# Three-pass fp32 feed-forward stages: 18 of 22 gate/up units as 2x2 block products with seven products for eight

## The reference, cut to what matters

```python
D_MODEL, SEQ, FFN_HIDDEN = 1024, 512, 2816

def swiglu(h, w1, w3, w2):
    return (jax.nn.silu(h @ w1) * (h @ w3)) @ w2
...
        h = modulate(rms_norm(x), sh2, sc2)
        x = x + g2[:, None, :] * swiglu(h, ffn_w1[layer], ffn_w3[layer], ffn_w2[layer])
```

## Time and profile before

| | |
|---|---|
| runs, us | 2479.25, 2486.27, 2486.68 |
| profiled execution, span, us | 2481.9 |
| PE busy | 2416.7 us, 97% of the span, 12256 matmuls |
| DVE, ACT, POOL busy | 1238.3 us (50%), 902.1 us (36%), 70.3 us (3%) |
| mean granted TensorE clock | 0.986 of full speed |
| DMA | 267.34 MB, mean 108 GB/s |

### The profile page before, as it was taken

One profiled execution on the slowest core, in us unless ns is written; L12 is line 12 of the kernel. 1 busy time (PEld: TensorE's weight loads), 2 busy tenths in 40 slices (PEclk: granted clock), 3 DMA queues, 4 the chain that ended last, 5 costly groups with the idle time before them and its releaser, 6 DMA issues.

```text
span 2481.9 us, 30237 instructions
## 1 busy us (share of the span) xinstructions
PE 2416.7 (97%) x12256; PEld 2022.5 (81%) x12256; DVE 1238.3 (50%) x1449; ACT 902.1 (36%) x1215; POOL 70.3 (3%) x81
## 2 busy tenths in 40 slices
PE   7989999999999999999999999999999999999998
PEld 6658888888799778888878888879989877888886
DVE  6677543356746543332254442346678545444423
ACT  3353333313344333332143332244556544333311
POOL 0210000000003000000000000000000000000000
PEclk9999999999999999999999999999999999999999
DMA  8116522364233122222222222221212212222221
GB/s 341 73 63 243 186 102 101 139 239 164 87 123 91 68 84 86 101 101 100 87 85 101 98 88 102 102 98 69 85 52 79 75 68 85 85 101 101 88 100 67
DMA packets 40549, 267.34 MB, mean 108 GB/s; under 512 B 4394, under 2 KB 5674, under 8 KB 9490
## 3 DMA queue, kind: packets, MB, share of 16 engines
q1 hardware_dynamic: 31248, 219.87, 24.6%
q0 software_dynamic: 5840, 40.37, 4.2%
q10 hardware_dynamic: 3378, 5.91, 0.9%
HBM read 263.90 MB, written 2.24 MB: 107 GB/s over the span
## 4 chain that ended last, share of the span: by engine, by line
PE 89%; DVE 6%; ACT 3%; issue 1%; DMA 0%; DVEq 0%; SPq 0%; ACTq 0%
PE bank L231 26%; PE bank L233 26%; PE bank L232 26%; DVE w_lo L218 1%; PE bank L2160 1%; ACT w_hi L214 1%; PE bank L2256 1%; PE bank L334 1%; PE bank L2243 1%; PE bank L1868 1%; DVE work L461 1%; DVE work L445 1%; PE bank L2231 1%; PE bank L1864 1%; ACT work L438 1%
## 5 line engine op out<-in xcount | busy, mean ns | idle before, releaser
L231 PE MATMUL bank<-h_hi,w_hi 128*128 128x512 f32 x1800 | 711.1, 395 | 5.3 <-DVE w_lo L218 2.0
L233 PE MATMUL bank<-h_hi,w_lo 128*128 128x512 f32 x1800 | 703.3, 391 | 0.0
L232 PE MATMUL bank<-h_lo,w_hi 128*128 128x512 f32 x1800 | 703.3, 391 | 0.0
L218 DVE TENSOR_TENSOR w_lo<-raw,w_hi 128x2048 fp32r<-128x2048 f32 x192 | 439.9, 2291 | 477.6 <-ACT w_hi L214 477.6
L214 ACT ACTIVATE w_hi<-raw 128x2048 fp32r<-128x2048 f32 x192 | 366.3, 1908 | 413.1 <-PE bank L233 409.6
L231 PEld LDWEIGHTS bank<-h_hi,w_hi 128*128 128x128 f32 x1800 | 339.5, 189 | 82.0 <-issue 6.7
L233 PEld LDWEIGHTS bank<-h_hi,w_lo 128*128 128x128 f32 x1800 | 339.4, 189 | 71.8
L232 PEld LDWEIGHTS bank<-h_lo,w_hi 128*128 128x128 f32 x1800 | 339.7, 189 | 70.6 <-issue 1.4
L233 PE MATMUL bank<-g_hi,w_lo 128*128 (+1 forms) x704 | 273.9, 389 | 0.0
L231 PE MATMUL bank<-g_hi,w_hi 128*128 (+1 forms) x704 | 273.9, 389 | 0.0
L232 PE MATMUL bank<-g_lo,w_hi 128*128 (+1 forms) x704 | 273.9, 389 | 0.0
(11 more groups left out here) (331 smaller groups left out, 2816.9 us busy)
## 6 DMA issues: line engine op xcount, KB each, us to landing
raw<-stream SPq DMA_DIRECT2D x192, 1024.0 KB, 4.8
work<-stream POOLq DMA_DIRECT2D x19, 1024.0 KB, 6.5
h_plain<-stream POOLq DMA_DIRECT2D x16, 1024.0 KB, 5.4
work<-stream SPq DMA_DIRECT2D x13, 1024.0 KB, 12.3
work<-mlstm_rows ACTq DMA_DIRECT2D x8, 512.0 KB, 4.8
x<-xT SPq DMA_DIRECT2D x1, 2048.0 KB, 10.5
outT<-work SPq DMA_DIRECT2D x8, 256.0 KB, 2.3
work<-mlstm_rows ACTq DMA_DIRECT2D x8, 192.0 KB
```

Source lines behind the costliest of these rows:

```text
L218: nc.vector.tensor_tensor(w_lo[:, slot(m), :], raw[:, slot(m), :], w_hi[:, slot(m), :], ALU.subtract).then_inc(lo_split, 1)
L231: nc.tensor.matmul(out, stationary[0], moving[0], start=first, stop=False)
L232: nc.tensor.matmul(out, stationary[0], moving[1], start=False, stop=False)
L233: return nc.tensor.matmul(out, stationary[1], moving[0], start=False, stop=last)
```

## The change

The first four gate/up units (`FFN_WHOLE`) stay as they are. In the other 18 of each stage the 128 gate columns and the 128 up columns, the even and the odd chunks of the 1024 features, and the two halves of the tokens (256 and 256) make a 2x2 by 2x2 block product. It is computed by a scheme with seven products (Winograd's form) instead of eight. A product is 4 chunks x 3 passes = 12 matmuls of 256 columns.

- **Sums of h**, five per stage, each 128 x 4 x 256, plus in ffn2 and ffn3 eight multiplications of x by the gain: on POOL, in place in `t` (`FeedForward.gpsimd`). They start when h (or x) is complete. ACT and DVE split the result into `t_hi_tile` and `t_lo_tile` (`hidden_high`, `hidden_low`), behind unit 0's work in their queues.
- **Sums of weights**, four per unit: two by an accumulating DMA that POOL issues (`add_parts`, 512 KB added to 512 KB loaded in `mixes`), two by DVE (`make_further`). SP issues three DMAs per unit instead of one (512, 256 and 512 KB).
- **Splits**: three weight blocks from raw (`whole_high`, `whole_low`, 1536 columns), two from `mixes` and two from `further` (1024 columns each). `w_hi` and `w_lo` hold one unit's seven blocks, so the buffer is single.
- **Sums of results**: ACT copies one product (`keep_first`), DVE makes four additions (`add_first`, `add_last`) over PSUM and SBUF, then the gate (`gate_chunk`); ffn2 and ffn3 have one multiplication by `inv_rows` more.
- **g** is kept whole in SBUF and split in pairs of chunks during the down units through three small buffers (`scale_pair`, `pair_high`, `pair_low`).
- The loops of these stages are written out; several semaphores are merged, which changes no wait in substance. In ffn0 the `add_unit` calls stand at every second fast unit, and POOL's loads of `ada_w` come between its accumulating DMAs.

```diff
+            def load(self, sp, m):
+                q, r, s = self.QUARTER, m - self.fast(0), slot(m)
+                sp.wait_ge(lo_split, m - 1)
+                src = stream[place_of(m), :, :]
+                sp.dma_start(raw[:, s, 0:2 * q], src[:, 0:2 * q]).then_inc(landed[s], 16)
+                sp.dma_start(raw[:, s, 2 * q:3 * q], src[:, 3 * q:]).then_inc(landed[s], 16)
+                sp.wait_ge(part_lo, self.hidden_lows(2) if r < 2 else self.part_low("mixes", r - 2))
+                sp.dma_start(self.mixes[s], src[:, q:3 * q]).then_inc(landed[s], 16)
+            def add_parts(self, pool, r):
+                q, s = self.QUARTER, slot(self.fast(r))
+                pool.wait_ge(landed[s], landings(self.fast(r)))
+                pool.dma_start(self.mixes[s], stream[place_of(self.fast(r)), :, 2 * q:], accum_op=ALU.add).then_inc(
+                    mixed_in[s], 16)
+            def gpsimd(self, pool):
...
+                for i, (out, one, two) in enumerate(((b11, b12, b11), (b12, b22, b12), (b21, b22, b21), (b22, b11, b22),
+                                                     (b21, b21, b11))):
+                    nc.gpsimd.tensor_tensor(out, one, two, ALU.subtract).then_inc(hidden_sums, 1)
+                    pool.wait_ge(hidden_sums, self.sums_base + self.sums_first + i + 1)
...
             def scalar(self, act, st):
...
+                self.mixes_high(act, 0)
+                for r in range(FAST):
+                    self.further_high(act, r)
+                    if r:
+                        self.apply(act, r - 1)
+                    if r + 1 < FAST:
+                        self.whole_high(act, r + 1)
+                    self.keep_first(act, r)
+                    if r + 1 < FAST:
+                        self.mixes_high(act, r + 1)
+                self.pair_high(act, 0)
+                act.wait_ge(products, self.product_done(4, FAST - 1))
+                split_hi(act, self.md)
+                self.apply(act, FAST - 1)
+                self.pair_high(act, 1)
+                split_hi(act, self.md + 1)
...
             def vector(self, dve, st):
...
+                for r in range(FAST):
+                    self.further_low(dve, r)
+                    if r:
+                        self.add_last(dve, r - 1)
+                    if r + 1 < FAST:
+                        self.make_further(dve, r + 1)
+                    if r:
+                        self.gate_chunk(dve, r - 1)
+                    if r + 1 < FAST:
+                        self.whole_low(dve, r + 1)
+                        self.mixes_low(dve, r + 1)
+                    else:
+                        self.scale_pair(dve, 0)
+                        self.pair_low(dve, 0)
+                        self.scale_pair(dve, 1)
+                        split_lo(dve, self.md)
+                    self.add_first(dve, r)
+                    if self.ada and r and r % 2 == 0 and r < 16:
+                        conditioning.add_unit(dve, 3 * KC + r // 2)
+                self.add_last(dve, FAST - 1)
+                self.gate_chunk(dve, FAST - 1)
...
+            def plain_products(self, pe, r):
+                n = self.HALF
+                pe.wait_ge(lo_split, self.fast(r) + 1)
...
+                self.product(self.begin(r)[:, 0:n], self.block("a11"), self.plain(0, 0), True, True)
+                self.product(self.middle(r)[:, 0:n], self.block("a12"), self.plain(1, 0), True, True)
+                self.product(self.ends(r)[:, n:], self.block("a22"), self.mixed(1, 0), True, True).then_inc(products, 1)
...
             def tensor(self, pe):
...
+                pe.wait_ge(part_lo, self.hidden_lows(2))
+                for r in range(FAST):
+                    self.plain_products(pe, r)
+                    self.mixes_products(pe, r)
+                    self.further_products(pe, r)
...
+                if self.ada:
+                    pe.wait_ge(conditioning.mod_done, 4)
+                for d in range(FB // 2):
...
+                    for k, o in order:
+                        if first and k == 0 and o == early[0]:
+                            pe.wait_ge(halves_added, self.added(4, late - 1))
+                        if first and k == 0 and o == after[0]:
                             pe.wait_ge(gated, self.j0 + FB)
```

More of the change, by code:

```diff
@@ L207, in place_of, with landings @@
             return ADA_UNITS + m
+        def landings(m):
+            done = m // 2 + 1
+            for name in ("ffn0", "ffn1", "ffn2", "ffn3"):
+                first = FIRST_UNIT[name] + FFN_WHOLE
+                done += 2 * sum(n % 2 == m % 2 for n in range(first, min(m + 1, first + FB - FFN_WHOLE)))
+            return 16 * done
         def split_hi(act, m, i=0):
-            act.wait_ge(landed[slot(m)], 16 * (m // 2 + 1) + 16 * i)
+            act.wait_ge(landed[slot(m)], landings(m) + 16 * i)
             if m >= 2:
@@ new lines, in rescale @@
+                    dve.wait_ge(silu_done, self.j0 + j + 1)
+                    nc.vector.tensor_tensor(self.chunk(j), self.silu[:, j % 2, :], bank[:, b + 1, :],
+                                            ALU.mult).then_inc(gated, 1)
+                self.hidden_bias(dve)
+                for j in range(self.CONV):
+                    rescale(j)
+                    if j < 2:
+                        split_next_lo(dve, self.m0 + j)
+                    if j == 0:
+                        self.hidden_low(dve)
+                    if j == self.CONV - 2:
+                        self.make_further(dve, 0)
+                        self.whole_low(dve, 0)
@@ new lines, in vector @@
+                self.add_last(dve, FAST - 1)
+                self.gate_chunk(dve, FAST - 1)
+                if self.ada:
+                    conditioning.write_mod(dve, st, 3)
+                self.pair_low(dve, 1)
+                split_lo(dve, self.md + 1)
+                for d in range(FB // 2 - 1):
+                    if d < FB // 2 - 2:
+                        self.scale_pair(dve, d + 2)
+                        self.pair_low(dve, d + 2)
+                    split_next_lo(dve, self.md + d)
+                    if self.ada and 1 <= d < 9:
+                        conditioning.add_unit(dve, 4 * KC + 2 * d - 2)
+                        conditioning.add_unit(dve, 4 * KC + 2 * d - 1)
@@ L804, in early_unit, with product @@
                 return last
[L806 to L813 removed]
+            def product(self, out, weights, moving, first, last):
+                wh, wl = weights
+                for p in range(KC // 2):
+                    c = slice(p * P, p * P + P)
+                    ins = three_passes(out, (wh[:, c], wl[:, c]), moving(p), first and p == 0, last and p == KC // 2 - 1)
+                return ins
@@ new lines, in further_products @@
+            def further_products(self, pe, r):
+                n = self.HALF
+                pe.wait_ge(part_lo, self.part_low("further", r))
+                self.product(self.middle(r)[:, n:], self.block("s2"), self.mixed(1, 1), True, True).then_inc(products, 1)
+                self.product(self.ends(r)[:, 0:n], self.block("s4"), self.plain(1, 1), True, True).then_inc(unit_used, 1)
+            def tensor(self, pe):
+                for j in range(self.CONV):
+                    m = self.m0 + j
+                    pe.wait_ge(lo_split, m + 1)
+                    if j >= 2:
+                        pe.wait_ge(gated, self.j0 + j - 1)
+                    if j == 0 and self.norm.deferred:
```

507 lines of the change are left out of this document (349 added, 158 removed).

## The result

The changed kernel takes 2495.73 us (median of 7 runs, 2487.95 to 2501.32), the kernel before 2483.19 us in the 7 runs beside and before it (2479.25 to 2487.34). The ratio is 1.0048, 95% interval 1.0032 to 1.0064: **0.5% slower**. The profiled execution has a span of 2493.9 us against 2481.9, 12.0 more. The forecast was no change at 2486; the time is 0.4% above that and inside the range, but the interval lies wholly beyond 0.3% on the slower side. That side had a chance of 0.36, no change had 0.34, and of the 0.36 only 0.08 lay within my own account.

The account below looks back on a forecast made before the run. PE, busy 97% of the span, was taken as the bound. Gain -57.6 plus 7.4, 1.4, 11.3, 2.6, 23.7 and 11.2 sum to 0.0; span 2481.9 with 4.4 more for the median of runs gives 2486 us, range 2466 to 2535.

Parts of the forecast that it names:

- gain: PE's fast units: 84 matmuls of 256 columns take 10.08 us instead of 10.88, over 72 units 57.6 us less.
- unit 3 of ffn0 and ffn1: Start of both stages: PE waits for unit 3's silu and weight splits, queued behind POOL's sums and h's split, 3.7 us each.
- first plain products: Start of ffn0 and ffn1: mixes load waits for hidden_low, so whole_low ends after PE is ready, 0.7 us each.
- squares of ffn2: Start of ffn2: DVE's additions of squares take turns with POOL's sums, so PE waits 11.3 us more.
- start of ffn3: Two additions behind POOL sums delay the row product 1.6 us; w_lo of unit 1 moves behind a third, 1.0 more.
- ends: Ends of the fast loops: PE waits around the first down matmuls, 7.8 us ffn0, 4.5 ffn1, 5.7 each ffn2 and ffn3.
- clock: After each of seven new waits above 3 us, a 3.4 us half-clock stretch costs 1.6: 11.2 us, bounds 0 and twice that.
- A: Fast loops: the accumulating DMA's time from issue to landing, taken as 6.6 us; up to 9 it fits in two unit periods.
- The 7: Fast loops: time in us for a unit's 1.25 MB of loads to land, counted from whole_low of two units earlier.
- Rival 1: Accumulating DMA paces the fast loops, making make_further wait; at A = 11, 70 us more, time 2556; chance 0.22.
- Rival 3: DVE bounds the fast loops, at 0.1 us more per operation: 20 us slower, time 2506; chance 0.06.
- Rival 2: Stage edges cost less: POOL sums of 1.6 us, no half-clock stretches after new waits, 20.6 us less, time 2465; chance 0.17.

Follow-up runs that it names:

- experiment 7: Kernel before, only PE's 18 gate/up units per stage cut to 84 matmuls of 256 columns, no sums or new DMAs, result incomplete: 2424.61 us, ratio 0.9762.
- experiment 1: Changed kernel with the accumulating DMA adding only 64 of its 1024 columns: 2471.62 us, ratio 0.9956 to the kernel before.
- experiment 2: Changed kernel with SP loading the 512 KB that is added to first, POOL waiting for it alone: 2472.47 us, ratio 0.9955 to the kernel before.
- experiment 6: Changed kernel with the first pair of g split one step earlier and, in ffn0, write_mod before the last gate: 2486.42 us, ratio 1.0011 to the kernel before.
- experiment 4: Changed kernel with ACT and DVE splitting the sums of h behind unit 1's work, not unit 0's: 2499.74 us, ratio 1.0073 to the kernel before.
- experiment 8: Changed kernel with loads reordered, sums after squares, sums split later with own place for first two loads, first pair earlier: 2441.90 us, ratio 0.9834 to the kernel before.

## Why the prediction was wrong

| term | forecast | measured |
|---|---|---|
| gain | -57.6 | -57.9 (experiment 7) |
| unit 3 of ffn0 and ffn1 | 7.4 | 6.5 |
| first plain products | 1.4 | 0 |
| squares of ffn2 | 11.3 | 8.05 |
| start of ffn3 | 2.6 | 0 |
| ends | 23.7 | 17.5 |
| in the loops | 0 | 17.9 in brackets (24.7 from start to start; 23.5 by experiment 1) |
| clock | 11.2 | 14.3, of which 11 at the edges |
| sum | 0.0 | 6.4, and 5.6 not in these terms: 1.7 ahead of the changed stages, the rest what waits cost beyond their brackets |

**The step that failed is the weight DMAs.** It said "11.1 + A <= 20.2, **A up to 9**" with 7 us until the loads have landed and an accumulation of 6.6, both constant, and so put the waits in the loops at nothing. They cost 17.9 us in brackets and 24.7 from start to start, twice the 12.0 by which the kernel got slower. Two things were wrong in the sum.

- The 7. From the end of `whole_low` of unit r-2 to the issue of the accumulation it takes 9.1 us in the median. That leaves A up to 7.0, not 9.
- The constant A. The median of 5.8 was even below my 6.6, but an accumulation and SP's loads for the next unit go out in the same period, and when they do so within 0.7 us the accumulation takes 7.2 to 10.0: 24 of 72. The rest, 6.5 and less, mostly had room.

The sum of the medians, 4.1 + 9.1 + 5.8 = 19.0, still says that it fits; for the unit ahead of 2303.23 it is 4.1 + 10.3 + 10.0 = 24.4. I had compared rates (175 of 218 GB/s), which are averages over a period. In a calm part of the loop, 1390 to 1480 us, the DMAs move 182 GB/s, and the row of 1369.00 shows 323: neither 218 as the full rate nor the average was the right thing to compare. Rival 1 named the place exactly, "the wait of make_further, with gate and whole_low queued behind it", but tied it to one constant A that decides from 9 on, with a cost of 61 in the loops at 11. So its place came true and its condition did not.

**The gain** was right to 0.3 us, from ten starts of matmuls of the same shape. By the gap that the Trainium skill (TensorE: Matmul & The Clock Gate, Back-to-back issue gap) states for an isolated matmul, the estimate was 85; experiment 7 measures 57.9, so the trace's distance was the right one to take.

**DVE in a unit** was right: the durations are as interpolated (1.75, 1.22, 0.69, 0.42), and in experiment 1, with no late transfer, PE never waits for DVE in a loop. Rival 3 is out.

**The starts.** Unit 3 was right in place, cause and size (3.25 each for 3.7). POOL's sums are slower than I took, 2.64 in the median for 2.2 (2.4 where nothing stands in their way), and the gain multiplications take 1.57 for 0.5 to 1.1; yet PE's wait for the squares of ffn2 grew by 8.05 only: the gain multiplications still ran when the last x came, the first additions were through before the first sum began, and the last one ended at 1274.20, after four sums and not five. The 0.7 ahead of the first plain products did not come; probably the stall of unit 3 gives the DMAs the same time, and I had counted both. It is close: in ffn1, experiments 2 and 6 have 2.73 and 1.72 there. In ffn3 the two additions were done before the row product was due.

**The ends** were right in order and cause, 17.5 for 23.7: ffn1 3.0 + 1.5 measured 2.67 and nothing, ffn0 7.8 measured 6.92, ffn2 and ffn3 5.7 each measured 4.8 and 3.1. The last gate of ffn1, to cost 1.5, came in time.

**The clock.** One stretch for each wait above 3 us was nearly right at the edges (11 for 11.2), though two were of 6.8 us. That it does not come from the new shape is shown by experiment 7. Some waits went without a stretch (3.14 at 1503.84) and one of 2.58 had one, so "above 3 us" is no rule; and the earlier trace rows, from which I took it, had eight one-column matmuls ahead of the stretch besides the wait, which the kernel before shows to be enough at 355.3, when there are 32.

**Rival 2** was right only in that the edges cost less, 14 less than forecast. Its reason, sums of 1.6 us, was wrong (they take 2.4 and more), and so was its clock. That the time is within 0.4% of the forecast is luck: errors of 14 down at the edges and 21 up (17.9 in the loops, 3.1 of clock) partly cancelled.

## What to carry to other kernels

When two transfers in series must fit in a period, don't add their medians: lay the issue times of all queues beside each other, and price each transfer at what it takes when they coincide. Count from the event that starts the chain, not from the issue of its last part. Let the transfer that another one waits for go first, ahead of waits that belong to its neighbours only. And for a change that makes matmuls fewer, count each edge against the bare gain: here edges and waits cost 70 us against a gain of 58, in a handful of places, each of which an edit of a few lines could shrink.

## What was not expected of the hardware

- In the kernel after, an accumulating DMA of 512 KB takes 5.3 to 6.5 us from issue to landing when SP's nearest load is 1.0 us or more away, not more than the plain load of the same size from another source in the earlier trace rows (6.6), and 7.2 to 10.0 when a load goes out within 0.7 us of it. With another order of the loads (experiment 2) the line is less sharp: one of 9.1 has its nearest load 2.2 us away.
- GpSimd takes 2.39 to 4.48 us (median 2.64) for a difference of two operands of 1024 columns, and 1.57 for a multiplication of 512 columns by a per-partition factor, which has one tensor operand; DVE takes 1.22 for the first.
- After a wait of 2.6 to 7 us PE works at half clock for 3.4 or 6.8 us, not after every such wait; in experiments 4, 6 and 8 also after waits of 1.8 to 2.2, and in the kernel before after 32 one-column matmuls without a wait. Where PE still waits in part of the stretch, as from 491.7 to 493.4, that part costs nothing.
- In the loops of fast units a wait costs 0.25 us more from start to start than the idle time that the trace shows before the matmul.
